# Moving the weight sums of the late units from VectorE to GpSimd

## The reference, cut to what matters

```python
z = rmsnorm(h, norm_g)
proj = jnp.einsum('btd,de->bte', z, w_in)                 # 1024 -> 9 x 1024 columns
u_a = a_val * jax.nn.sigmoid(a_glu)
c_a, new_buf_a = causal_dwconv(buf_a, u_a, conv_a_w)      # 31 taps
c_a = layernorm(c_a + conv_a_b, ln_a_g, ln_a_b)
y_a = jax.nn.silu(c_a) * jax.nn.silu(a_gate)
c_b, new_buf_b = causal_dwconv(buf_b, b_c * b_h, conv_b_w)  # 3 taps
y_b = b_b * c_b * jax.nn.silu(b_gate)
merged = (jax.nn.sigmoid(m_a) * jnp.einsum('btc,cd->btd', y_a, w_pa)
          + jax.nn.sigmoid(m_b) * jnp.einsum('btc,cd->btd', y_b, w_pb))
h = h + jnp.einsum('btd,de->bte', merged, w_out)
y = rmsnorm(h, final_norm_g)
```

## Time and profile before

| | |
|---|---|
| median of 3 runs | 1069.04 us (1068.72 to 1070.01) |
| the profiled execution's own time | 1069.02 us |
| its span in the trace | 1067.2 us |
| PE busy | 1025.9 us, 96% |
| DVE busy | 829.4 us, 78% |
| POOL busy | 519.0 us, 49% |
| ACT busy | 471.8 us, 44% |

### The profile page before, as it was taken

One profiled execution on the slowest core, in us unless ns is written; L12 is line 12 of the kernel. 1 busy time (PEld: TensorE's weight loads), 2 busy tenths in 40 slices (PEclk: granted clock), 3 DMA queues, 4 the chain that ended last, 5 costly groups with the idle time before them and its releaser, 6 DMA issues.

```text
span 1067.2 us, 19847 instructions
## 1 busy us (share of the span) xinstructions
PE 1025.9 (96%) x7948; PEld 998.0 (94%) x7948; DVE 829.4 (78%) x904; ACT 471.8 (44%) x725; POOL 519.0 (49%) x369
## 2 busy tenths in 40 slices
PE   5899999999999999999999999799998988999997
PEld 5899999999999999999999999799998988998885
DVE  6779989899998989899996674875595489765523
ACT  7654343434434343433444555556463354242311
POOL 3166566565655656566563553445564456420000
PEclk9999999999999999999999999899998999999999
DMA  8677666657656665665656464584946646455321
GB/s 266 173 163 182 153 170 156 170 128 192 154 149 175 157 168 130 186 157 147 173 149 204 140 211 138 180 272 156 316 149 216 211 120 208 154 195 177 119 81 41
DMA packets 183535, 181.03 MB, mean 170 GB/s; under 512 B 9135, under 2 KB 145455, under 8 KB 182404
## 3 DMA queue, kind: packets, MB, share of 16 engines
q1 hardware_dynamic: 168468, 152.50, 44.5%
q0 software_dynamic: 14976, 27.27, 14.2%
HBM read 118.46 MB, written 35.00 MB: 144 GB/s over the span
## 4 chain that ended last, share of the span: by engine, by line
PE 85%; DVE 5%; DMA 3%; ACT 3%; issue 2%; POOL 1%; SPq 1%; ACTq 0%; DVEq 0%
PE pp L2020 74%; PE pp L2180 8%; DMA sgb<-m_spill 2%; DVE big L1506 1%; DVE xop L1469 1%; PE pp L2037 1%; POOL wop L918 1%; PE spare L2196 1%; DVE big L1948 1%; ACT wop L1017 1%; DVE ring L1664 1%; DVE x_stage L1458 1%; DMA x_stage<-in_x_prompt_dram 1%; ACT wop L985 0%; ACT xop L1001 0%
## 5 line engine op out<-in xcount | busy, mean ns | idle before, releaser
L2020 PE MATMUL pp<-xop,wop 128*128 128x262 f32 (+1 forms) x7224 | 892.1, 285 | 22.1 <-issue 7.5
L2020 PEld LDWEIGHTS pp<-xop,wop 128*128 128x128 f32 x7224 | 885.3, 190 | 26.8 <-issue 15.8
L918 POOL TENSOR_TENSOR wop<-ring,wop 128x512 fp32r<-128x512 f32 (+1 forms) x256 | 442.4, 1733 | 389.3 <-ACT wop L985 384.8
L985 ACT ACTIVATE wop<-ring 128x512 fp32r<-128x512 f32 (+1 forms) x262 | 181.6, 698 | 233.0 <-PE pp L2020 232.9
L1575 DVE SCALAR_TENSOR_TENSOR big<-big,cst 128x513 f32<-128x513 f32 x112 | 107.8, 963 | 0.7
L2180 PE MATMUL pp<-xop,wop 128*128 128x512 f32 x384 | 89.2, 394 | 0.0
L2180 PEld LDWEIGHTS pp<-xop,wop 128*128 128x128 f32 x384 | 72.0, 188 | 16.8
L1586 DVE SCALAR_TENSOR_TENSOR spare<-big,tap_sum,spare 128x512 f32<-128x512 f32 x112 | 83.7, 748 | 0.3
L1575 DVE SCALAR_TENSOR_TENSOR spare<-big,cst,spare 128x512 f32<-128x512 f32 x112 | 83.6, 746 | 0.0
L1677 DVE TENSOR_TENSOR big<-big,pp 128x524 f32<-128x524 f32 (+1 forms) x43 | 29.8, 693 | 45.9 <-PE pp L2020 45.1
L1664 DVE TENSOR_TENSOR ring<-ring 128x512 f32<-128x512 f32 x68 | 64.3, 985 | 0.0
(11 more groups left out here) (127 smaller groups left out, 713.5 us busy)
## 6 DMA issues: line engine op xcount, KB each, us to landing
ring<-in_w_in_dram SPq DMA_DIRECT2D x222, 256.0 KB, 3.3
ring<-ring POOLq DMA_DIRECT2D x104, 256.0 KB, 4.4
big<-c_spill SPq DMA_DIRECT2D x16, 516.0 KB, 5.1
big<-yb_spill SPq DMA_DIRECT2D x5, 1032.0 KB, 9.5
big<-ya_spill SPq DMA_DIRECT2D x5, 1032.0 KB, 8.0
m_spill<-big SPq DMA_DIRECT2D x16, 262.0 KB, 4.4
yb_spill<-big SPq DMA_DIRECT2D x8, 516.0 KB, 5.4
c_spill<-big SPq DMA_DIRECT2D x8, 516.0 KB, 4.5
```

What stands on the lines that cost most here:

```text
L918: G.tensor_tensor(wop[:, s0:s1, 1, :], raw, f(wop[:, s0:s1, 0, :]), ALU.subtract).then_inc(wlo, 1)
L985: A.activation(wop[:, s0:s1, 0, :], raw, ACT.Copy).then_inc(whi, 1)
L2020: last = T.matmul(out, wop[:, s, wp, P * k:P * (k + 1)], xop[s][:, xp, k, n * ch:n * (ch + 1)], start=(s in FRESH and k == 0 and m == 0), ...
```

## The change

`weight_sum(v, n)` is taken out of VectorE's program and written, with the same semaphores waited for and the same one counted, into GpSimd's. There it stands between the low parts: sum 0 of unit u + 1 behind `w_lo(u, 5)` and ahead of `w_lo(u + 1, 0)`, sum 1 ahead of `w_lo(u + 1, 1)`, sums 2 and 3 ahead of `w_lo(u + 1, 2)`. It concerns the 17 units 27 to 43, so 68 additions. No other engine's program is changed.

```diff
--- before.py
+++ after.py
@@ -917,6 +917,28 @@
                 raw, s0, s1 = w_step(v, n)
                 G.tensor_tensor(wop[:, s0:s1, 1, :], raw, f(wop[:, s0:s1, 0, :]), ALU.subtract).then_inc(wlo, 1)
 
+            def weight_sum(v, n):
+
+                u1, u3 = u13[v % 2][:, 0, :], u13[v % 2][:, 1, :]
+                if n == 0:
+                    pool.wait_ge(rb11_in, 16 * (v + 1))
+                    pool.wait_ge(u13_in[v % 2], u13_at(v))
+                    pool.wait_ge(wlo, w_at(v - 2, 3))
+                    if v - 2 < VSUM:
+                        pool.wait_ge(a2, 16 * (v - 2))
+                else:
+                    pool.wait_ge(usum, usum_at(v, (0, 0, 0, 1)[n]))
+                if n == 1:
+                    pool.wait_ge(rb22_in, 16 * (v + 1))
+                    pool.wait_ge(wlo, w_at(v - 1, 2))
+                    if v - 1 < VSUM:
+                        pool.wait_ge(a4, 16 * (v - 1))
+                if n == 3:
+                    pool.wait_ge(rb21_in, 16 * (v + 1))
+                    pool.wait_ge(wlo, w_at(v - 1, 5))
+                out, x, y = ((u1, rb11, u3), (u2, u1, rb22), (u3, u3, rb22), (u4, u2, rb21))[n]
+                G.tensor_tensor(out, x, y, ALU.add).then_inc(usum, 1)
+
             for n in range(4):
                 w_lo(0, n)
 
@@ -930,16 +952,24 @@
 
             for u in range(1, NU):
                 v = u + 1
+                sums = VSUM <= v < NU
                 if u > 1:
                     w_lo(u, 5)
+                if sums:
+                    weight_sum(v, 0)
                 if v < NU:
                     w_lo(v, 0)
                 if v < VSUM:
                     u3_sum(v)
+                if sums:
+                    weight_sum(v, 1)
                 if v < NU:
                     w_lo(v, 1)
                 if v < VSUM:
                     u4_sum(v)
+                if sums:
+                    weight_sum(v, 2)
+                    weight_sum(v, 3)
                 if v < NU:
                     w_lo(v, 2)
                 if v + 1 < VSUM:
@@ -1641,28 +1671,6 @@
                 dve.wait_ge(cb_step, 5 * j + 4)
                 V.tensor_reduce(cbuf[:, SEQ:TOK], sbw[:, :, :], mybir.AxisListType.X, ALU.add).then_inc(cb_step, 1)
 
-            def weight_sum(v, n):
-
-                u1, u3 = u13[v % 2][:, 0, :], u13[v % 2][:, 1, :]
-                if n == 0:
-                    dve.wait_ge(rb11_in, 16 * (v + 1))
-                    dve.wait_ge(u13_in[v % 2], u13_at(v))
-                    dve.wait_ge(wlo, w_at(v - 2, 3))
-                    if v - 2 < VSUM:
-                        dve.wait_ge(a2, 16 * (v - 2))
-                else:
-                    dve.wait_ge(usum, usum_at(v, (0, 0, 0, 1)[n]))
-                if n == 1:
-                    dve.wait_ge(rb22_in, 16 * (v + 1))
-                    dve.wait_ge(wlo, w_at(v - 1, 2))
-                    if v - 1 < VSUM:
-                        dve.wait_ge(a4, 16 * (v - 1))
-                if n == 3:
-                    dve.wait_ge(rb21_in, 16 * (v + 1))
-                    dve.wait_ge(wlo, w_at(v - 1, 5))
-                out, x, y = ((u1, rb11, u3), (u2, u1, rb22), (u3, u3, rb22), (u4, u2, rb21))[n]
-                V.tensor_tensor(out, x, y, ALU.add).then_inc(usum, 1)
-
 
             def c11(u):
                 dve.wait_ge(prod, prod_at(u, 1))
@@ -1831,8 +1839,6 @@
                     w_low(5)
                 if u > 1:
                     after_c21(u - 1)
-                if VSUM <= u + 1 < NU:
-                    weight_sum(u + 1, 0)
                 if kind == "gate":
                     conv_b(i)
                 if spread:
@@ -1864,9 +1870,6 @@
                     x_low(1, 5)
                 if u == NPB:
                     x_low(2, 5)
-                if VSUM <= u + 1 < NU:
-                    for step in (1, 2, 3):
-                        weight_sum(u + 1, step)
                 if kind == "gate":
                     sample_b(i)
                 if spread:
```

## The result

The changed kernel takes 1087.62 us (median of 4 runs, 1086.51 to 1090.48), the kernel before 1069.53 us in the same comparison (1068.72 to 1071.81): a ratio of 1.0157, 95% interval 1.0139 to 1.0175 (the two medians alone give 1.0169, inside it). It is 17 to 18 us slower; the prediction was 1085 us. The profiled execution has a span of 1085.9 us against 1067.2, so +18.7 us in the trace.

What follows compares the result with a forecast made beforehand. TensorE, busy 96%, was taken as the bound, so time comes only from idle places, lower clock or new waits. -0.5 + 7.5 + 0.4 + 8.5 = +15.9 us on 1069.0 gave 1085 us, range 1077 to 1095.

Steps and rivals of the forecast that it cites:

- Turns: VectorE instructions with two on-chip inputs and GpSimd's exclude each other and alternate; a sum takes 1.29 instead of 0.68 us.
- Ordinary units, price 0: Units 27 to 34, 38, 41 to 43: sums fit GpSimd's idle time, price 0; with one gain, -0.5 us.
- The chain to 673: Chain to TensorE's start at 673.08: the sum at 668.07 leaves it, gaining 0.3 to 0.7 us.
- First phase change, +7.5: Units 35 to 38: turns delay GpSimd's low parts and sums and the loads queued behind them; +7.5 us.
- the upper of the two ends: First phase change, units 35 to 38: chain late by 6.7 to 8.4 us; 8.4 is the upper end.
- may add 2 at each new gap: TensorE's half clock behind new gaps may add 2 us each; counted only in the range, to 1095.
- Second phase change, +0.4: Units 39 and 40: turns end x_low 6 at 900.5 instead of 900.0, +0.4 us.
- Merge, +8.5: Unit 41: load_old(0), queued behind load_rb21, and GpSimd's turns delay the merge and slot 3; +8.5 us.
- the middle of 5.4 and 11.6: Merge, slot 3 of unit 41: lateness between 5.4 us and 11.6 with GpSimd's turns and lower clock; middle taken, +8.5.
- Relief of VectorE at no cost: Rival: chains through VectorE at the phase changes shorten with no price at the exclusion, 6.8 us go, 1062; chance 0.12.
- Only the first change loses: Rival: only the first phase change costs, the merge ending about when slot 3 is due; 1076.5 us, chance 0.22.

Runs made afterwards that it cites:

- the fillings: Changed kernel with each weight sum on GpSimd replaced by a write-only filling of the same block, some 1.3 us: 1067.91 us, ratio 0.9962 to the kernel before.
- the experiment where the load comes early: Changed kernel with load_old(0) moved on SyncE ahead of load_rb11 and load_rb21 of unit 42: 1080.38 us, ratio 1.0086 to the kernel before.
- the units 40 and 41 alone: Changed kernel with only units 40 and 41's sums on GpSimd, all others back on VectorE: 1077.41 us, ratio 1.0053 to the kernel before.

## Why the prediction was right, step by step

- **Turns.** The central step held: the two engines exclude each other and alternate. Low 4 of unit 36 ended at 797.1, 799.0 was forecast. That it is exclusion and not the longer program is shown by the fillings of the same length: 0.9962 against 1.0157.
- **Ordinary units, price 0.** Right: 1.0012 (0.9991 to 1.0033) with 13 units on GpSimd. The chain to 673 gave 0.6 us of idle (-0.5 forecast). The 0.50 us of the gap at 783.84 was a gain that the sum didn't have.
- **First phase change, +7.5.** Slot 2 of unit 38 was 8.7 us late, 8.4 more than at 673, which is the upper of the two ends (8.4). Each station was close: load_rb22 of unit 38 at 817.8 (818.5), first_product 824.6 (823.4 to 824.8), the end of sum 3 at 832.0 (831 to 832.5). One link was misread: the long gap falls on slot 4 of unit 36, not slot 5. `third_product` waits for a spill (7.64 us) that stands behind load_rb22 too, one step ahead of the stage buffer's load that the prediction named. At the end of unit 36 the products were therefore 5.2 us late and not 2.3 (3.1 by the prediction's own numbers: with slot 5 at 809.3, slot 6 starts at 812.2, where before had 809.16): two waits, and 2.6 us of lower clock between them. The size at slot 2 of unit 37 still came out nearly the same (5.3, forecast 4 to 5), because that slot waits for the next stage load, which stands behind the same chain.
- **What the sum left out.** Unit 39's slot 2 was 10.7 us late, 2.0 more. Of this 1.4 is the lower clock: the chain of waits runs through TensorE's slots from 849.76, and load_rb22 is issued 15.4 us behind them (865.16) where before took 14.0 (841.06 to 855.02); the other 0.6 is the stage load behind it. The matmuls behind 825.31 and 874.07 take 1.4 to 1.5 us longer as well, but TensorE then waits 2.45 and 1.51 us for ScalarE, so these don't show as lateness. The prediction had the clock only as something that "may add 2 at each new gap" and put it into the range.
- **Second phase change, +0.4.** Measured 9.6 less 10.7, so -1.1 us: the idle time of 4.1 us in before (1.30, 0.92 and 1.91) became 1.9 (1.51 and 0.35), and the lower clock takes part of that back. GpSimd wasn't without a gap from 864 to 910 as forecast: it waited for ScalarE 2.76 us ahead of 874.52 and 3.02 ahead of 896.96.
- **Merge, +8.5.** Measured 17.1 less 9.6, so +7.5. load_old(0) was 16.6 us later in time, 5.9 to 7.0 against the products (7.3 forecast: 7.7 less 0.4), and took 7.2 us until VectorE began, not 5.4. The wait that was forecast ahead of slot 3 of unit 41 (3 us or more) fell for the most part on slot 2 (3.91 us, for `first_product` behind the first multiplication), with 1.83 left for slot 3. The turns in the merge, which the prediction had at up to 4 us, showed only in the experiment where the load comes early; their upper end was also added up 1.4 us short (some 5 us and six turns of 1.29 are 12.7, not 11.3; that experiment measured 11.4), as was the end of sum 3 by 0.4 (864 and 40.9 are 904.9). So the place and the load were right, but that the middle of 5.4 and 11.6 came within 1.0 us is in part luck: the turns and the lower clock that it averaged in didn't fill it; the late load did, with a landing 1.7 us slower.
- **The sum.** Forecast +15.9, measured +18.1 in the medians and +18.7 in the trace. The terms in the trace are 0.9 of late start, which isn't the change's, -0.6 ahead of 673, +10.4 from there to slot 2 of unit 39, -1.1, +7.5, and 1.5 more up to w_out, which is the lower clock behind 928.95 (53.90 us, where the same matmuls took 52.4 in before: 64.09 less four slots). Against the forecast these are 2.9 us more up to unit 39, 1.5 and 1.0 less at the second change and the merge, and 1.5 more at the end, so the total is nearer than its parts: errors cancel in it.
- **The rivals.** Relief of VectorE at no cost is worth 4.7 us, but the change doesn't have it at no cost. "Only the first change loses" is refuted by the units 40 and 41 alone (1.0053).

## What to carry to other kernels

Before an elementwise operation moves from VectorE to GpSimd, count in the busiest stretch, not on average, how much time both engines spend on instructions that read two operands in on-chip memory: these take turns, and the operation now costs 1.29 instead of 0.68 us of the common time. Then read in the transfer queue what is issued behind the loads that wait for GpSimd; here some 14 of 17 us of the loss went through that order, and moving a few loads ahead of those waits gave the kernel before as much (0.9953) as leaving the sums out altogether (0.9956).

## What the runs showed of the hardware

Instructions of VectorE with both inputs in on-chip memory and GpSimd's additions or subtractions alternate one by one under load: 3.36 us for a GpSimd instruction of 1.29 that meets one of 2.25 on VectorE, again and again. A filling on GpSimd, which only writes, isn't part of this: 0.52 us for 128x512 beside x_low instructions. The Trainium skill, "SBUF — State Buffer", section "Who interferes with whom", has this as well: a VectorE instruction with two SBUF inputs contends with a GpSimd instruction that reads SBUF, not with one that only writes it; the trace of the experiment with the fillings agrees.

Not expected was that gaps of TensorE much under the 4.33 and 6.17 us of before can be followed by its lower clock level (1.2 of 2.4 GHz) too: behind 2.02, 2.37 and 2.45 us of idle in the changed kernel the windows show a granted clock of 0.67 to 0.72, while behind the 1.77 and 1.91 us of before it was 1.00. The length of the last gap doesn't decide it alone: behind 1.83 us ahead of 928.95, where 3.91 us of idle and a single slot had gone before, it was 0.67, and in the kernel with the fillings it was 1.00 behind 2.48 us (ahead of 841.71). The matmuls behind such a gap take some 1.4 us longer; that is lost on top of the gap where the chain of waits runs through them, as in unit 38, and hidden where TensorE waits for another engine next.
